# Latents by token ahead of the SSM inputs, and two orders of ACT's work, in a hybrid mixer and expert kernel

## The reference

```python
h = rms_norm(x, mix_norm)
c_q, c_kv, k_pe, u_ssm, conv_a, conv_g = split(h @ w_in)      # 256, 128, 32, 256, 256, 256 columns
q  = rms_norm(c_q, q_a_norm) @ w_uq                           # 8 heads of 96
kv = rms_norm(c_kv, kv_a_norm) @ w_ukv                        # 8 heads of 64 + 64
q, k = rms_norm(q, q_norm), rms_norm(concat(k_nope, k_pe), k_norm)   # then rotary, chunk-causal attention
y_ssm  = z * sigmoid(z @ w_glu), z = gelu(S5 scan of u_ssm + d * u_ssm)
y_conv = silu(layer_norm(depthwise_conv31(conv_a * sigmoid(conv_g))))
x = x + concat(rms_norm(y_attn), rms_norm(y_ssm), rms_norm(y_conv)) @ w_out
x = x + hier_moe(rms_norm(x, ffn_norm))                       # 32 experts, top 2 of a group of 8
```

## Time and profile before

| | us |
|---|---|
| median of 3 runs | 1255.36 (1254.25 to 1255.47) |
| the profiled execution | 1256.61 |
| its span, first to last instruction | 1254.5 |
| PE busy | 1130.0 (90%) |
| DVE busy | 978.3 (78%) |
| ACT busy | 700.2 (56%) |
| POOL busy | 378.5 (30%) |
| mean granted TensorE clock | 0.965 of 2.4 GHz |
| first scores of the attention start at | 258.98 |

### The profile page before, as it was taken

The page is one execution under the profiler, slowest core; times in us unless marked ns, Lnnn a source line. Parts: engine busy times, 40 slices in busy tenths (PEclk is TensorE's granted clock), DMA queues, the critical chain, the costliest instruction groups (busy, mean ns, idle before and its releaser), DMA issues.

```text
span 1254.5 us, 15926 instructions
## 1 busy us (share of the span) xinstructions
PE 1130.0 (90%) x5636; PEld 866.9 (69%) x5636; DVE 978.3 (78%) x1182; ACT 700.2 (56%) x818; POOL 378.5 (30%) x359
## 2 busy tenths in 40 slices
PE   4899999688888889996699999999999999999992
PEld 3447565555666568785588888888887887787771
DVE  1979999846655646367799999999998998899971
ACT  5521225544454643223377777777777777777751
POOL 2304007376854000011212233332333333243220
PEclk9999999899999999997799999999999999999996
DMA  6700000000005000337599999999999999999930
GB/s 198 169 0 1 0 10 18 2 0 1 2 1 231 5 34 2 123 129 272 216 388 366 370 395 373 394 400 377 380 383 380 372 364 366 373 355 369 362 129 10
DMA packets 55485, 260.93 MB, mean 208 GB/s; under 512 B 31089, under 2 KB 31761, under 8 KB 41617
## 3 DMA queue, kind: packets, MB, share of 16 engines
q1 hardware_dynamic: 45344, 243.03, 50.5%
q0 software_dynamic: 10096, 17.34, 5.7%
HBM read 252.25 MB, written 26.35 MB: 222 GB/s over the span
## 4 chain that ended last, share of the span: by engine, by line
PE 60%; DVE 19%; DMA 9%; issue 4%; ACT 4%; SPq 2%; POOL 0%; DVEq 0%; ACTq 0%; POOLq 0%
PE psum L2112 26%; PE psum L2132 11%; DMA w<-in_w 9%; PE psum L2024 6%; DVE arena L1305 6%; DVE arena L1107 5%; PE psum L1972 3%; PE psum L1942 2%; PE psum L1758 2%; PE psum L1960 2%; PE psum L2102 2%; DVE am L1435 1%; PE psum L2118 1%; PE psum L1928 1%; DVE arena L1110 1%
## 5 line engine op out<-in xcount | busy, mean ns | idle before, releaser
L1602 DVE TENSOR_TENSOR w_rest<-w,w_high 128x2048 fp32r<-128x2048 f32 x136 | 305.3, 2286 | 18.3 <-ACT w_high L1028 18.0
L1028 ACT ACTIVATE w_high<-w 128x2048 fp32r<-128x2048 f32 x136 | 256.4, 1913 | 73.0 <-DMA w<-in_w 52.8
L2112 PE MATMUL psum<-w_high,xgT_high 128*128 128x512 f32 x544 | 217.5, 400 | 12.2 <-DVE xgT_rest L1648 12.1
L2112 PE MATMUL psum<-w_rest,xgT_high 128*128 128x512 f32 x544 | 213.7, 393 | 0.0
L2112 PE MATMUL psum<-w_high,xgT_rest 128*128 128x512 f32 x544 | 213.3, 392 | 0.0
L1655 DVE TENSOR_TENSOR w_rest<-w,w_high 128x2048 fp32r<-128x2048 f32 x68 | 152.5, 2284 | 1.8 <-ACT w_high L1038 1.8
L1038 ACT ACTIVATE w_high<-w 128x2048 fp32r<-128x2048 f32 x68 | 126.3, 1908 | 20.3 <-DMA w<-in_w 20.2
L691 POOL DMA_INDIRECT out<-arena,idx x34 | 91.7, 2697 | 123.6 <-DVE arena L1668 118.3
L2112 PEld LDWEIGHTS psum<-w_high,xgT_high 128*128 128x128 f32 x544 | 102.9, 189 | 37.2 <-issue 14.3
L2112 PEld LDWEIGHTS psum<-w_rest,xgT_high 128*128 128x128 f32 x544 | 102.9, 189 | 22.0
L2112 PEld LDWEIGHTS psum<-w_high,xgT_rest 128*128 128x128 f32 x544 | 103.1, 190 | 20.4
(11 more groups left out here) (269 smaller groups left out, 2032.0 us busy)
## 6 DMA issues: line engine op xcount, KB each, us to landing
w<-in_w SPq DMA_DIRECT2D x102, 2048.0 KB, 18.0
arena<-in_x SPq DMA_DIRECT2D x5, 1024.0 KB, 4.9
h_scratch<-arena SPq DMA_DIRECT2D x8, 512.0 KB, 2.6
out<-arena SPq DMA_DIRECT2D x8, 512.0 KB, 3.6
arena<-in_x SPq DMA_DIRECT2D x1, 3072.0 KB, 20.5
arena<-in_w_in SPq DMA_DIRECT2D x1, 2688.0 KB, 14.9
arena<-in_w_in SPq DMA_DIRECT2D x1, 2048.0 KB, 12.3
wout_y_raw<-in_w_out SPq DMA_DIRECT2D x1, 2048.0 KB, 9.9
```

What stands on the lines that cost most here:

```text
L1028: act.activation(w13h[k][:, c, :], w13[b][k][:, c, :], ACT.Copy).then_inc(W13H_READY[k], 1)
L1602: dve.tensor_tensor(w13l[b][k][:, c, :], w13[b][k][:, c, :], w13h[k][:, c, :].bitcast(F32), S_).then_inc(W13_SPLIT[k], 1)
L2112: last = pe.matmul(psum[:, k, :], x_[:, c, :], w_[:, c, :], start=(c == 0 and n == 0), stop=(c == KC - 1 and n == 2))
```

## The change

The latents are projected by token, 384 columns in one bank for each tile (`project_latents`), ahead of the SSM inputs. ACT squares each tile with a sum along the row, POOL makes the two roots of the tile at once, ACT saves the tile scaled by them (`save_latents`), and PE transposes four tiles at a time (`turn_latents`) into `cqT` and `ckvT`. The tiles lie in `latt`, partly where `utok` is written later. The matmuls with ones, the separate squares and the scale at `save_qkv` go. POOL's scaling of `wuq` and `wukv` stands behind the eight roots. At the query root ACT makes both halves of z, loads the root's table with a square root of one column, saves the turned z, and only then waits for `qk_mean`; silu follows. In the front ACT works in two halves and serves the first half of `save_ag` ahead of the long sines, and PE turns C before the second half's projections.

The diff, cut:

```diff
         sigT = at(19772, 2, T)
-        sqc = at(14336, 3, T)
+        latt = [at(S0 + 4096 + (QL + KL) * i if i < 3 else S0 + (QL + KL) * (i - 3), QL + KL) for i in range(NT)]
         cacc = at(YT0 + 2048, 2, T)
+        squares_q, squares_k = at(YT0 + 1024, QL), at(S0 + 1920, KL)
...
-        F_U = lambda i: 2 * NT + 8 + i
-        F_LAT = lambda half, m: 3 * NT + 8 + 3 * half + m
-        F_SSQ = 3 * NT + 14
-        F_QKV = lambda i, k: F_SSQ + 1 + 4 * i + k
+        F_LAT = lambda i: 2 * NT + 8 + i + (3 if i >= 6 else 0)
+        F_U = lambda i: 3 * NT + 11 + i + (3 if i >= 2 else 0)
+        F_TURN = lambda half, m: (2 * NT + 14 if half == 0 else 3 * NT + 13) + m
+        F_QKV = lambda i, k: 4 * NT + 14 + 4 * i + k
...
             pool.wait_ge(wproj_in, 16 * 3)
+            for i in range(NT):
+                pool.wait_ge(lat_squared, i + 1)
+                mean, root = st[:, 16 + 2 * i:18 + 2 * i], st[:, 32 + 2 * i:34 + 2 * i]
+                link(pool.tensor_scalar(root, mean, 1.0, EPS, ALU.mult, ALU.add))
+                pool.tensor_tensor(root, root, minus_half[:, 0:2], ALU.pow).then_inc(lat_rms, 1)
+
             for c in range(2):
                 pool.tensor_scalar(wuq[:, c, :], wuq[:, c, :], normc[:, 2 * KC + c:2 * KC + c + 1], None, ALU.mult)
             pool.tensor_scalar(wukv, wukv, normc[:, 2 * KC + 2:2 * KC + 3], None, ALU.mult).then_inc(wproj_scaled, 1)
-
-            pool.wait_ge(lo_drained, F_SSQ + 1)
-            rms(16, 32, QL, NT, EPS, lat_rms)
-            rms(24, 40, KL, NT, EPS, lat_rms)
...
+            for half in range(2):
+                i0 = 4 * half
+                square_x(i0)
+                for i in range(i0, i0 + 4):
+                    if i + 1 < i0 + 4:
+                        square_x(i + 1)
+                    scale_x(i)
+                    if half == 0 and i >= 1:
+                        save_xT(i - 1)
+                if half == 0:
+                    save_xT(3)
 
             act.wait_ge(trig_ready, 1)
             act.activation(sc[:, 7, :], sc[:, 5, :], ACT.Sin, scale=0.5)
             act.activation(sc[:, 8, :], sc[:, 5, :], ACT.Sin).then_inc(trig_done, 1)
+            for m in range(2):
+                save_ag(0, m)
+            for i in range(4, NT):
+                save_xT(i)
             act.wait_ge(consts_made, 1)
             act.wait_ge(phase_ready, 1)
...
-
-            save_ag(0)
-            for i in range(4, NT):
-                save_xT(i)
-            save_ag(1)
+            for m in range(2):
+                save_ag(1, m)
 
...
             act.wait_ge(ssm_w_ready, 1)
+
+            def save_latents(i):
+                bank = lo(F_LAT(i))
+                act.wait_ge(lo_filled, F_LAT(i) + 1)
+                act.activation(squares_q, bank[:, 0:QL], ACT.Square, scale=QL ** -0.5, accum_out=st[:, 16 + 2 * i:17 + 2 * i])
+                act.activation(squares_k, bank[:, QL:QL + KL], ACT.Square, scale=KL ** -0.5,
+                               accum_out=st[:, 17 + 2 * i:18 + 2 * i]).then_inc(lat_squared, 1)
+                act.wait_ge(lat_rms, i + 1)
+                act.activation(latt[i][:, 0:QL], bank[:, 0:QL], ACT.Copy, scale=st[:, 32 + 2 * i:33 + 2 * i])
+                act.activation(latt[i][:, QL:QL + KL], bank[:, QL:QL + KL], ACT.Copy,
+                               scale=st[:, 33 + 2 * i:34 + 2 * i]).then_inc(lo_drained, 1)
+
+            def save_turned(half):
+                act.wait_ge(upad_ready, 4)
+                for m in range(3):
+                    n = F_TURN(half, m)
+                    act.wait_ge(lo_filled, n + 1)
+                    dst = cqT[:, m, :] if m < 2 else ckvT
+                    act.activation(natural(dst, half), lo(n).rearrange("p (i j) -> p i j", i=4), ACT.Copy).then_inc(lo_drained, 1)
+
+            for i in range(NT):
+                save_latents(i)
+                if i == 5:
+                    save_turned(0)
             for i in range(NT):
                 n = F_U(i)
+                if i == 2:
+                    save_turned(1)
                 act.wait_ge(lo_filled, n + 1)
...
-            act.wait_ge(upad_ready, 4)
-            for half in range(2):
-                for m in range(3):
...
-            act.wait_ge(lo_drained, F_LAT(1, 2) + 1)
-            for m in range(3):
-                last = act.activation(sqc[:, m, :], cqT[:, m, :] if m < 2 else ckvT, ACT.Square)
-            last.then_inc(lat_squared, 1)
-            act.wait_ge(lo_filled, F_SSQ + 1)
-            act.activation(st[:, 16:16 + 2 * NT], lo(F_SSQ)[:, 0:2 * NT], ACT.Copy).then_inc(lo_drained, 1)
-
-            act.wait_ge(lat_rms, 2)
...
-                    act.activation(qraw[:, i, k * 384:k * 384 + 384], lo(n)[:, 0:384], ACT.Copy,
-                                   scale=st[:, 32 + i:33 + i]).then_inc(lo_drained, 1)
+                    act.activation(qraw[:, i, k * 384:k * 384 + 384], lo(n)[:, 0:384], ACT.Copy).then_inc(lo_drained, 1)
...
-                                              v[:, :, d0:d0 + ND], ACT.Copy, scale=st[:, 40 + i:41 + i])
+                                              v[:, :, d0:d0 + ND], ACT.Copy)
...
             save_z(0)
-            act.wait_ge(qk_mean, 1)
-            act.activation(at(14336 + 2816, 2 * NT * H), qks.rearrange("p a i h -> p (a i h)"), ACT.Sqrt).then_inc(qk_root, 1)
             link(save_z(1))
             act.sem_inc(z_ready, 1)
             act.sem_inc(hi_drained, 1)
-            act.wait_ge(ln_done, 1)
-            act.activation(ctok, ctok, ACT.Silu).then_inc(conv_act_done, 1)
+            act.activation(tmp[:, 0:1], ones[:, 0:1], ACT.Sqrt)
             act.wait_ge(hi_filled, R_Z + 1)
             for k in range(4):
                 last = act.activation(zT.rearrange("p c (k i j) -> p k i c j", k=4, i=2)[:, k],
                                       psum[:, 4 + k, :].rearrange("p (i c j) -> p i c j", i=2, c=2), ACT.Copy)
             last.then_inc(hi_drained, 1)
+            act.wait_ge(qk_mean, 1)
+            act.activation(at(14336 + 2816, 2 * NT * H), qks.rearrange("p a i h -> p (a i h)"), ACT.Sqrt).then_inc(qk_root, 1)
+            act.wait_ge(ln_done, 1)
+            act.activation(ctok, ctok, ACT.Silu).then_inc(conv_act_done, 1)
...
             for half in range(2):
                 turn_x(half)
+                if half == 1:
+                    pe.wait_ge(ssm_par_in, 16 * 11)
+                    hi(R_C)
+                    for k in range(2):
+                        last = pe.transpose(psum[:, 4, k * P:(k + 1) * P], C2[:, k, :], ident[:, :])
+                    last.then_inc(hi_filled, 1)
                 pe.wait_ge(win_ag_scaled, 1)
...
-            pe.wait_ge(ssm_par_in, 16 * 11)
-            hi(R_C)
...
             pe.wait_ge(win_scaled, 1)
+
+            def project_latents(i):
+                bank = lo(F_LAT(i))
+                for c in range(KC):
+                    last = pe.matmul(bank[:, 0:QL + KL], hT[:, c, i, :], win[:, c, CQ0:KPE0], start=(c == 0), stop=(c == KC - 1))
+                last.then_inc(lo_filled, 1)
+
+            def turn_latents(half):
+                pe.wait_ge(lo_drained, F_LAT(4 * half + 3) + 1)
+                for m in range(3):
+                    bank = lo(F_TURN(half, m))
+                    for i in range(4):
+                        last = pe.transpose(bank[:, i * P:(i + 1) * P], latt[4 * half + i][:, m * P:(m + 1) * P], ident[:, :])
+                    last.then_inc(lo_filled, 1)
+
             for i in range(NT):
+                project_latents(i)
+                if i == 5:
+                    turn_latents(0)
+            for i in range(NT):
+                if i == 2:
+                    turn_latents(1)
...
-            for half in range(2):
-                for m, c0 in enumerate((CQ0, CQ0 + P, CKV0)):
-                    project(F_LAT(half, m), half, c0)
...
-            pe.wait_ge(lat_squared, 1)
-            bank = lo(F_SSQ)
-            for i in range(NT):
-                for m in range(2):
-                    pe.matmul(bank[:, i:i + 1], sqc[:, m, i * P:(i + 1) * P], ones[:, 0:1], start=(m == 0), stop=(m == 1))
-                last = pe.matmul(bank[:, NT + i:NT + i + 1], sqc[:, 2, i * P:(i + 1) * P], ones[:, 0:1], start=True, stop=True)
-            last.then_inc(lo_filled, 1)
+            pe.wait_ge(lo_drained, F_TURN(1, 2) + 1)
             pe.wait_ge(wproj_scaled, 1)
```

31 lines of the change are left out of this document (8 added, 23 removed).

## The result

The changed kernel took 1306.32 us in the median of four runs (1302.17 to 1308.13), the kernel before 1255.41 beside it (1254.25 to 1262.88). The ratio is 1.039 (95%: 1.036 to 1.043). The profiled execution took 1305.47 us, with a span of 1303.4 against 1254.5. The forecast was 1245.1, with a range of 1240 to 1252.

A forecast was written before the change was run, and what follows sets the result against it. It took DVE's chain up to the root, then ACT and PE up to the first scores, as the bound. Scores 11.1 us earlier, less 0.8 for low clock, gave 10.3 off 1255.36: 1245.1 us, range 1240 to 1252.

The forecast's parts named there:

- Part 2: Latents by token on PE: V ends at 180.0 and DVE starts the SSM at 180.1, 3.2 us earlier.
- Rival E: Latent tiles' round trip: POOL's small operations each wait two taps (2.5 us); 10.5 us net lost, 1265.9; chance 0.05.
- rival C: Beside the taps: POOL's scaling of wuq blocks them in full, 7.5 us lost from the sum, 1252.6; chance 0.10.
- Part 1: Front: C's wait goes, DVE's block starts 5.9 us earlier, and the taps end at 175.25 instead of 182.35.
- The 4 us of the front: Front's share of the predicted 10.3 us gain, about 4 us, beside 6 from the root.
- rival D: Front gives nothing, V or the taps ending where they did; only the root's order pays, 1249.3; chance 0.15.
- Part 3: Query root: PE turns head 0 at 243.35 instead of 255.37; scores start at 247.9 instead of 258.98; about 6 us gained.
- The carrying over: After the first scores: later work waits only for its own earlier work, so their shift reaches the end unchanged.

The follow-up runs named there:

- the repaired version: The changed kernel with every fourth convolution tap on DVE waiting for the end of the tap just before it; 1250.40 us, ratio 0.998.
- the version where 37.87 us of waiting cost nothing: The changed kernel with latents saved unscaled, POOL making all 16 roots at once, applied when queries, keys and values are saved; 1252.12 us, ratio 0.996.

## Why the prediction was wrong

**The step that failed is in Part 2: "one wait of PE at latent 6, for ACT's answer to latent 5 ... I estimate 2.9 in all, less 1.4 of turns ...: +1.4".** The wait was 49.09 us, and it came earlier in the order than that, at the first turn of latents, for tile 3; V ended at 236.8 (233.08 + 3.71), where I had 180.0. I had priced POOL's two operations by a mean over forms (0.86) that came from stretches where DVE ran nothing like the taps. No row of before showed a small POOL read beside the taps: POOL was idle from 108.72 (104.13 + 4.59) to 187. That was an unshown operation on the path, and I put a single figure where a bound was due.

**Rival E had the mechanism and not the size.** It said that POOL's small operations have to wait for the taps because these leave no gap, and put two taps ahead of each, 2.5 us. So it reached 1265.9, and a chance of 0.05. Its evidence against (the 1.64 of the power at 189.33 beside one two-input operation) stood beside loose operations, not in a row that overlaps. The rule of the Trainium skill ("SBUF — State Buffer", section "Who interferes with whom") named the pair rightly. I turned it only against DVE, in rival C, and it was POOL that lost. As I read it, with the lock held for one instruction at a time, a wait would be at most one tap, 1.28 us. That holds for the additions that were let in and for none of the five kept out: while the read of tile 3 waited, 46 more taps began one after the other.

**The rest of Part 2, held against the version with every fourth tap broken.** V ended at 183.4 (179.71 + 3.71), where I had 180.0. W was turned at 88.9 for 87.8 (DVE's own work ahead of it came 1.1 later); its turn took 3.65 for the 1.94 at the full clock (1.7, I took 1); the wait for the latents was 2.95 for 1.4. The turns (2 x 1.47) and the wait of V (2.15) were as I had them. The SSM so starts at 183.47, where it was at 183.32: on PE the latents by token use up all of the front's lead. PE's queries did begin 3.2 us earlier (183.35 for 186.55), a gain that I had rightly left out of the sum: DVE didn't wait for them before either.

**Part 1.** The mechanism was right: no wait for C, and taps that end at 172.7 (168.94 + 3.73) for 175.25. The scaling of the weights beside the taps cost some 2 us there (73.35 for 58 taps, against 69.4 and 14 waits of 0.11), within the 0 to 3 I took, and hidden; rival C is out. The 4 us of the front aren't there: the marker is at 252.92, and the root's order alone gives 254.04, no more apart than the marker's own scatter. By itself the front also gives nothing, by the rows for another reason (the latent roots beside the scan). That is rival D, 1249.3: the four versions with a broken row measured 1249.5 to 1255.0.

**Part 3** was right: forecast 6 us, measured 7.0 at the marker and 8.5 in the median (0.993). Two details. I had the root start as the mean comes; with the root's order alone, where the SSM came at its old time, DVE's reciprocal waited 3.50 us for it (0.43 before), since ACT stood in the save of turned z. And PE's turn of head 0 ran at the full clock there (1.95), and at the low one in the changed kernel (3.49), as I had it.

**The carrying over** held within the scatter of the tail: 45.4 us at the marker, 48.9 in the span, 50.9 in the median.

**How the 55 us become 45.4.** PE waited 49.09 where the repaired version has 2.95: 46.1 more. The low clock cost 2.5 in the tiles behind it (13.04 for 10.59; granted 0.84 from 180 to 192), and the tiles and turns around the wait the rest: V came 53.4 us later than repaired (233.08 - 179.71). Against the kernel before it is 53.5 - 8.1 = 45.4 at the marker.

**The lowest time is that of the root's order alone**, 1247.91 us (0.993, 0.990 to 0.996), below both kernels. With the latents by token as well, a break in the taps is needed, and then it is no better (0.995 to 0.999). The intervals just overlap, so an order among these versions isn't shown.

## What to carry to other kernels

Before a small GpSimd operation is put on the path beside a long row of VectorE operations that overlap, look for a row of the trace that shows the pair; without one, take the length of the whole row as the bound of its wait, not one operation. If a result must come from GpSimd there, break the row now and then (a wait for the instruction just before, 0.11 us), or keep the result off the path until the row is over, as in the version where 37.87 us of waiting cost nothing. And an earlier start of one engine is worth only what the next meeting point lets through: the front alone started the SSM 6.7 us earlier on DVE, and the marker stayed where it was (261.14 for 261.01).

## What the runs showed of the hardware that was not expected

- GpSimd reads of SBUF of one, two and sixteen columns were kept out for 17.83 to 60.18 us by VectorE operations that read two SBUF inputs and overlap by 0.08 us, while a memset (0.10) and an iota (0.14) passed, and while 24 one-column reads in a chain passed at 1.11 us each.
- VectorE's taps lost nothing to a small read: 58 of them took 69.45 us with the read of 55.46 us beside them, 69.44 without. With a wait at every fourth tap or more often in the row, none of 32 reads took over 1.28 us, though in the versions that left seams without a wait 17 of 24 ended at such a seam.
- TensorE's clock was granted at half (0.50, 1.2 GHz) in the window from 140 to 150, in its idle stretch, and was back at the full level in 192 to 200, after work began again at 173.93. Idle stretches of 2.95 and 3.04 us in two versions ended differently: granted 1.00 and 0.91 from 100 to 140, and 10.59 and 13.45 us for the same tiles behind them.
